# Moving splits and low parts among the units of a first mixer, with three neighbouring instructions swapped elsewhere

## The chip, the cores and the metric

One core of a Trainium2 chip runs the whole program as one launch. The metric is the device time of that launch in microseconds, the median of the runs shown.

## The reference

One layer of a bidirectional encoder for 512 tokens of 1024 channels. After an RMS norm one projection gives the inputs of two mixers and two gates; the mixers' outputs are projected, gated, summed, projected again and added to the input. Then an expert stage follows (16 experts, each takes its 64 best tokens), and a last norm. What the change touches is the first mixer, grouped-query attention with 8 query heads and 2 key heads of 64 channels:

```
h = rms_norm(x, norm1_g[l])
z = jnp.einsum('bsd,dn->bsn', h, w_in[l])
qa, ka, va, qb, kb, vb, ga, gb = jnp.split(z, splits, axis=-1)
...
s = jnp.einsum('bqkgd,bskd->bkgqs', qb, k).astype(jnp.float32)
p = jax.nn.softmax(s, axis=-1).astype(v.dtype)
return jnp.einsum('bkgqs,bskd->bqkgd', p, v)
```

## The kernel before, in words

**Numbers in two parts.** Large products are made of three matmuls: a float32 operand is split into a high part, rounded by ScalarE (ACT), and a low part, the rest, subtracted by VectorE (DVE). A product is high by high, high by low, low by high (`split_product`, L1158 to L1160). The weights w_in come in strips of 128 columns. A strip is loaded by the sync engine (SP) into a ring of four places, `split_hi` (ACT, L795) writes its high part, `split_lo` (DVE, L1878) its low part and counts `w_split` up. The load of a later strip into the same place waits for that count (`load_strip`, L568).

**The first mixer** runs as 32 units `u`, one for each head and each tile of 128 queries. Every engine has its own loop over the units:

- TensorE (PE, L1384): in its unit u the scores of unit u+2 (`scores_a`, L1315), in units 9, 17 and 25 a value product (`values_a`, L1357), then some steps of a column product (`fill`), then the turn, that is four transposes of the softmax rows of unit u (`turn_probs`, L1345).
- ACT (L917): the exponential of unit u (L879), then the read of the turned rows of unit u-2 (L891), then extras.
- DVE (L1998): the maximum of unit u's scores (L2001), then the reciprocal and scaling of unit u-1 (`norm_probs`, L1971 and L1973), then extras.

So DVE's unit u can begin as soon as PE has made the scores in its own unit u-2, and PE's turn of unit u waits for the normalisation in DVE's unit u+1.

**Column groups.** The steps of `fill` prepare queries and keys of the second mixer. There are seven groups of eight steps (three matmuls each); group g multiplies by strip 12+g. `A_FILL` (L469) says how many steps are done after each unit: groups 0 to 6 end in units 0, 5, 10, 15, 20, 25 and 30. The first step of a group waits for the low part of its strip, and for the bank it writes to be emptied (`col_steps`, L1218, through `wait_split` and `pp_take`). Group 2 starts with the second step of unit 5, groups 3, 4, 5 and 6 in units 10, 16, 21 and 26.

**The extras.** Once a group is full, its two heads are emptied: `high_col` on ACT (L902) writes a head's high part, `low_col` on DVE (L1980) its low part; a query head is one piece on each, a key head two pieces (DVE L1993, L1994). Further extras are the splits of the strips 14 to 19 and, four times, the output tile (`read_o`, `low_o`, DVE L1977). The tables `O_READ`, `O_LOW` and `A_LOWS` (L470, L471) name the units of the output tile and of the splits' low parts. The splits' high parts were placed by two conditions in the loop on ACT (L931 to L934).

**Other places.** Ahead of the mixer DVE writes the low parts of h (`low_hT`, L1871) and splits the first strips. The key heads of the first mixer get their low parts by `low_k` (L1918). Behind both mixers and the gates, tiles get their residual added (`add_residual`, L2094) and are routed (`route_max`, `route_norm`).

Of the kernel before, what the change touches and what calls it, by code (L numbers as in the profile page):

```python
# [38 lines left out]
KC = D // P  # L39
# [24 lines left out]
RING = 4  # L64
# [20 lines left out]
def encoder_block(nc, x, norm1_g, w_in, b_gates, q_norm_g, k_norm_g, w_o_a, w_o_b, w_out, norm2_g,  # L85
# [138 lines left out]
    with ExitStack() as ctx:  # L224
# [140 lines left out]
        NA = A_HEADS * NT  # L365
# [101 lines left out]
        N_COL_A = 2 * NG + 1  # L467
        A_LEAD = 6
        A_FILL = [min(N_COL_A * KC, A_LEAD + 2 + (i + 1) * (N_COL_A * KC - A_LEAD - 2) // (NA - 1)) for i in range(NA)]  # L469
        O_READ, O_LOW = (10, 19, 26), (11, 21, NA)  # L470
        A_LOWS = (2, 6, 10, 16, 20, 26)  # L471
        B_HIGHS, B_LOWS = (NA + 4, NA + 6, NA + 7), (NA + 6, NA + 7, NA + 8)
        B_FILL = ([2, 3, 4, 5, 7, 8, 8, 8], [3, 6, 7, 8, 11, 14, 16, 16])

# [15 lines left out]
        def filled_at(plan, g):  # L490

            return next(i for i, steps in enumerate(plan) if steps >= KC * (g + 1))

        def q_of(hp, hh, g):

# [268 lines left out]
        def _(act_):  # L764
# [19 lines left out]
            def split_hi(n):  # L784

                home, before = raw_home(n), before_in_home(n, part_home)
                arrived = sum(2 if strips[m][0] == "wo" else 1 for m in range(n + 1) if raw_home(m) == home)
                act_.wait_ge(w_raw_in[home], 16 * arrived)
                if part_home(n) != home:

                    act_.wait_ge(pv_done, OA + OB)
                elif before is not None:
                    wait_used(act_, before)
                raw, hi, _ = parts_of(n)
                act_.activation(hi, raw, ACT.Copy).then_inc(w_hi_done, 1)  # L795
# [121 lines left out]
            for u in range(NA + 4):  # L917
                if u < NA:
                    soft_exp(u, SEQ, pp[u % 3][:, :])
                    if u == 3 * NA // 4:  # L920

                        act_.dma_start(dist[:, :, :], distance).then_inc(dist_in, 16)
                if 2 <= u < NA + 2:
                    read_probs(u - 2)
                for g in range(N_COL_A):
                    filled = filled_at(A_FILL, g)
                    if u == (filled + 2 if g < N_COL_A - 1 else NA + 1):
                        high_col(g, 0)
                    if u == (filled + 3 if g < N_COL_A - 1 else NA + 1):
                        high_col(g, 1)  # L930
                    if u == filled + 4 and g < 2 * KC // RING:  # L931
                        split_hi(at[col_groups[g][1:]] + RING)
                if u in (1, 2):
                    split_hi(13 + u)  # L934
                if u in O_READ:
                    read_o(O_READ.index(u))

# [908 lines left out]
        def _(dve):  # L1846
# [21 lines left out]
            def low_hT(c):  # L1868
                dve.wait_ge(hT_hi_done, pieces_done(c))
                cols = slice(P * c, P * c + P)  # L1870
                dve.tensor_tensor(hT_lo[:, :, cols], turned_two[c % 2], hT_hi[:, :, cols].bitcast(F32),  # L1871
                                  ALU.subtract).then_inc(hT_lo_done, 1)
# [13 lines left out]
            low_hT(1)  # L1886
            norm_x(3)
            low_hT(2)
            low_hT(3)
            for n in range(2, 6):  # L1890
                split_lo(n)


# [24 lines left out]
            def low_k(kv):  # L1918

                dve.wait_ge(a_hi_done, a_read("k", kv))  # L1920
                half, other = halves_of(kv)
                src, high = tp[K_BANK][half, :], kA[half, kv, 0, :].bitcast(F32)
                dve.tensor_tensor(kA[half, kv, 1, :], src, high, ALU.subtract).then_inc(a_lo_done, 1)
                dve.tensor_tensor(kA[other, kv, 0, :], src, high, ALU.subtract).then_inc(a_lo_done, 1)
# [38 lines left out]
            low_q(2)  # L1963
            low_k(0)
            low_q(3)
            low_k(1)


            def norm_probs(u, width):
# [10 lines left out]
            def low_col(g, hh):  # L1980

                _, kind, grp, hp = col_groups[g]
                dve.wait_ge(col_hi_done, 2 * g + hh + 1)
                src = bank[bank_of[N_TOK + g]]
                half = slice(HD * hh, HD * hh + HD)
                other = slice(HD - HD * hh, 2 * HD - HD * hh)
                if kind == "q":
                    q = q_of(hp, hh, grp)
                    last = dve.scalar_tensor_tensor(q[other, :], src[half, :], SCALE / SLOPES[2 * hp + hh],
                                                    q[half, :].bitcast(F32), ALU.mult, ALU.subtract)  # L1990
                else:
                    hi = kB[half, hh, grp, 0, :].bitcast(F32)
                    dve.tensor_tensor(kB[other, hh, grp, 0, :], src[half, :], hi, ALU.subtract)  # L1993
                    last = dve.tensor_tensor(kB[half, hh, grp, 1, :], src[half, :], hi, ALU.subtract)  # L1994
                if hh:
                    last.then_inc(proj_read_dve, 1)

            for u in range(NA + 5):  # L1998
                if u < NA:
                    dve.wait_ge(score_done, u + 1)  # L2000
                    dve.tensor_reduce(column(nmax, u), pp[u % 3][:, :], AX, ALU.max, negate=True)\  # L2001
                        .then_inc(nmax_done, 1)
                if 1 <= u <= NA:
                    norm_probs(u - 1, SEQ)
                for g in range(N_COL_A):
                    filled = filled_at(A_FILL, g)
                    if u == (filled + 3 if g < N_COL_A - 1 else NA + 2):
                        low_col(g, 0)
                    if u == (filled + 4 if g < N_COL_A - 1 else NA + 3):
                        low_col(g, 1)  # L2010
                if u in A_LOWS:
                    split_lo(14 + A_LOWS.index(u))
                if u in O_LOW:
                    low_o(O_LOW.index(u))
# [99 lines left out]
            def route_norm(c):  # L2114

                dve.wait_ge(sexp_done, c + 1)
                settle(dve.reciprocal(sinv[:, c:c + 1], ssum[:, c:c + 1]))
                dve.tensor_scalar(aff[:, c, :], logit[:, c, :], sinv[:, c:c + 1], None, ALU.mult)\
                    .then_inc(aff_done, 1)


            def low_xn(c, h):

                dve.wait_ge(xn_hi_done, c + 1)
                cols = slice(SEQ * h, SEQ * h + SEQ)
                dve.tensor_tensor(xn_lo[:, c, cols].rearrange("p (k i) -> p k i", k=HALF),
                                  x2[:, c, cols].rearrange("p (i k) -> p k i", k=HALF),
                                  xn_hi[:, c, cols].rearrange("p (k i) -> p k i", k=HALF).bitcast(F32),
                                  ALU.subtract).then_inc(xn_lo_done, 1)
# [18 lines left out]
            route_max(1)  # L2148
            read_h2(2)
            low_xn(0, 1)  # L2150
            route_norm(0)
            add_residual(1, 3)
            low_xn(1, 0)
            low_xn(1, 1)
            read_h2(3, NT, HALF, KC - 2)
# [274 lines left out]
```

## Time and profile before

| | |
|---|---|
| three runs, median (lowest, highest) | 868.34 us (866.88, 869.37) |
| the profiled execution's own time | 867.77 us |
| its span, first to last instruction | 865.8 us |
| mean granted TensorE clock | 0.998 |
| PE busy | 842.6 us, 97% |
| DVE busy | 373.4 us, 43% |
| ACT busy | 264.1 us, 31% |

The page of the profile gives busy times for the whole span and groups instructions by line. The list of waits says for each engine what ended its idle time. The timeline lists single instructions or runs of equal ones in order of time; a number in square brackets behind one is the idle time of its engine just before it and what ended it. A busy PE is one whose records cover the time: matmuls overlap, so a record is longer than the distance to the next one. PEld are the weight loads of TensorE. All times are us from the span's start.

### The profile page before, as it was taken

The page shows a single profiled execution, that of the slowest core. Times are in us where ns is not written, and L with a number is a line of the kernel's source. Part 1 is how long each engine was busy: PE and PEld are TensorE (multiplying, and loading weights), DVE is VectorE, ACT ScalarE, POOL GpSimd, SP SyncE. Part 2 cuts the span into 40 slices and gives each one's busy share as a digit, 9 for nine tenths or more (in the row PEclk, how much of TensorE's full clock was granted, in tenths as well). Part 3 has the DMA queues.
Part 4 walks back from the last instruction along what each step waited for, and adds up shares of the span by engine and source line. Part 5 has one row for each costly group of instructions (what it writes and reads, how often), then busy time and mean ns, then how long its engine had stood idle before and what let it go on. Part 6 is the DMA issues. An engine that isn't in the chain of part 4 may idle for free.

```text
span 865.8 us, 10447 instructions
## 1 busy us (share of the span) xinstructions
PE 842.6 (97%) x4229; PEld 513.7 (59%) x4229; DVE 373.4 (43%) x648; ACT 264.1 (31%) x461; POOL 29.0 (3%) x50
## 2 busy tenths in 40 slices
PE   9999999999999999999999999999999998989996
PEld 8898766787878888888534343344433433334332
DVE  5377977676616245427322236223231311321351
ACT  6233866685624234216011010010100101001231
POOL 1050000000000000003000000000000000000010
PEclk9999999999999999999999999999999999999999
DMA  9730112023034335884899999999999999999995
GB/s 286 175 98 1 49 49 98 24 72 104 27 122 131 95 87 146 305 372 163 333 410 418 425 426 430 424 428 428 424 431 428 427 430 425 430 427 428 429 410 236
DMA packets 81428, 239.20 MB, mean 276 GB/s; under 512 B 8039, under 2 KB 63463, under 8 KB 66789
## 3 DMA queue, kind: packets, MB, share of 16 engines
q1 hardware_dynamic: 75952, 235.94, 69.2%
q10 hardware_dynamic: 5284, 2.09, 1.0%
q8 instruction: 34, 0.56, 0.3%
q0 software_dynamic: 144, 0.51, 0.1%
q14 instruction: 14, 0.11, 0.0%
HBM read 235.92 MB, written 2.62 MB: 276 GB/s over the span
## 4 chain that ended last, share of the span: by engine, by line
PE 82%; DMA 12%; DVE 3%; ACT 1%; issue 1%; POOLq 0%; POOL 0%; SPq 0%; ACTq 0%; DVEq 0%
PE psum L1645 18%; PE psum L1158 11%; PE psum L1677 11%; PE psum L1159 11%; PE psum L1160 11%; DMA wslot<-in_w_down 7%; DMA wslot<-in_w_up 4%; PE psum L1602 3%; PE psum L1696 2%; PE psum L1345 2%; PE psum L1357 2%; PE psum L1805 2%; PE psum L1331 2%; PE psum L1315 1%; PE psum L1164 1%; PE psum L1610 1%
## 5 line engine op out<-in xcount | busy, mean ns | idle before, releaser
L1645 PE MATMUL psum<-wslot,xinT 128*64 128x512 f32 x1000 | 222.4, 595 | 5.8 <-DMA wslot<-in_w_up 3.8
L1645 PEld LDWEIGHTS psum<-wslot,xinT 128*64 128x64 f32 x1000 | 69.8, 137 | 143.5 <-issue 132.1
L1677 PE MATMUL psum<-wslot,actT 128*64 128x512 f32 x424 | 96.0, 597 | 5.0 <-DMA wslot<-in_w_down 5.0
L1158 PE MATMUL psum<-hT_hi,w_hi 128*128 128x512 f32 x208 | 82.9, 399 | 0.0
L1160 PE MATMUL psum<-hT_hi,w_lo 128*128 128x512 f32 x208 | 81.2, 390 | 0.0
L1159 PE MATMUL psum<-hT_lo,w_hi 128*128 128x512 f32 x208 | 81.2, 390 | 0.0
L1878 DVE TENSOR_TENSOR w_lo<-w_raw,w_hi 128x1024 fp32r<-128x1024 f32 (+1 forms) x46 | 52.9, 1174 | 44.8 <-ACT w_hi L795 44.7
L1677 PEld LDWEIGHTS psum<-wslot,actT 128*64 128x64 f32 x424 | 29.2, 137 | 61.4 <-issue 57.4
L1091 ACT ACTIVATE actT<-psum 128x512 f32<-128x512 f32 x16 | 9.6, 597 | 174.4 <-PE psum L1657 174.4
L2283 DVE TENSOR_TENSOR x<-x,psum 128x512 f32<-128x512 f32 x48 | 29.7, 681 | 57.8 <-PE psum L1696 57.8
L2273 DVE TENSOR_TENSOR y_lo<-psum,y_hi 64x512 fp32r<-64x512 f32 x28 | 19.3, 689 | 81.1 <-ACT y_hi L1101 80.7
L795 ACT ACTIVATE w_hi<-w_raw 128x1024 fp32r<-128x1024 f32 (+1 forms) x46 | 45.2, 1017 | 16.3 <-PE psum L1160 16.3
L1158 PEld LDWEIGHTS psum<-hT_hi,w_hi 128*128 128x128 f32 x208 | 39.1, 188 | 10.1 <-issue 2.6
L1160 PEld LDWEIGHTS psum<-hT_hi,w_lo 128*128 128x128 f32 x208 | 39.0, 188 | 8.4
L1159 PEld LDWEIGHTS psum<-hT_lo,w_hi 128*128 128x128 f32 x208 | 39.1, 188 | 7.4
L1086 ACT ACTIVATE act<-psum,slot_vals 128x512 f32<-128x512 f32 x16 | 11.0, 687 | 93.3 <-PE psum L1645 93.3
L2260 DVE SCALAR_TENSOR_TENSOR act<-psum,slot_vals,act 128x512 f32<-128x512 f32 x16 | 12.0, 750 | 59.2 <-ACT act L1086 59.1
L891 ACT ACTIVATE pT<-psum 128x512 f32<-128x512 f32 x48 | 28.5, 596 | 23.6 <-PE psum L1345 13.3
L1101 ACT ACTIVATE y_hi<-psum 64x512 fp32r<-64x512 f32 x28 | 16.5, 589 | 57.3 <-PE psum L1677 57.0
L1602 PE MATMUL psum<-xn,pick 128*128 128x512 f32 x120 | 29.4, 396 | 0.0
L2226 DVE TENSOR_TENSOR xinT<-psum,small 128x512 f32<-128x512 f32 x15 | 9.7, 686 | 40.0 <-PE psum L1610 40.0
L2266 DVE SCALAR_TENSOR_TENSOR act<-act,slot_fac,psum 128x512 f32<-128x512 f32 x16 | 12.0, 747 | 32.8 <-PE psum L1645 32.8
(281 smaller groups left out, 1300.6 us busy)
## 6 DMA issues: line engine op xcount, KB each, us to landing
wslot<-in_w_up SPq DMA_DIRECT2D x27, 2048.0 KB, 25.3
wslot<-in_w_gate SPq DMA_DIRECT2D x25, 2048.0 KB, 26.7
wslot<-in_w_down SPq DMA_DIRECT2D x24, 2048.0 KB, 23.7
w_raw<-in_w_in SPq DMA_DIRECT2D x34, 512.0 KB, 4.3
wslot<-in_w_gate SPq DMA_DIRECT2D x12, 1024.0 KB, 9.5
wslot<-in_w_up SPq DMA_DIRECT2D x9, 1024.0 KB, 11.8
wslot<-in_w_down SPq DMA_DIRECT2D x9, 1024.0 KB, 7.7
w_raw<-in_w_out SPq DMA_DIRECT2D x8, 512.0 KB, 4.7
```

The source lines that it names most:

```text
L795: act_.activation(hi, raw, ACT.Copy).then_inc(w_hi_done, 1)
L891: last = act_.activation(pT[:, head % 2, :, cols], tp[(0, 3)[u % 2]][:, :].rearrange("p (k i) -> p k i", i=P), ACT.Copy)
L1158: pe.matmul(out_, s_hi, m_hi, start=(k == 0), stop=False)
L1159: pe.matmul(out_, s_hi, m_lo, start=False, stop=False)
L1160: return pe.matmul(out_, s_lo, m_hi, start=False, stop=(k == n_k - 1))
L1331: mm = pe.matmul(dst, q_of(head // 2, head % 2, g)[:, cols], keys, start=(v == 0), stop=(v == 1))
L1602: mm = pe.matmul(bank[6 + f][:, :], pick[:, c, :, :], part[:, c, cols], start=(c == 0 and part is xn_hi), stop=(c == NT - 1 and part is xn ...
L1645: mm = pe.matmul(bank[2 * e + n][CAP * f:CAP * f + CAP, :], xinT[:, HALF * h + k, CAP * e:CAP * e + CAP], wslot[place_of(m)][:, k % PART, ...
L1677: mm = pe.matmul(bank[4 + e][CAP * f:CAP * f + CAP, :], actT[:, e, k, CAP * h:CAP * h + CAP], wslot[place_of(m)][:, k % PART, SEQ * f:SEQ ...
L1878: dve.tensor_tensor(lo, raw, hi.bitcast(F32), ALU.subtract).then_inc(w_split, 1)
L2273: dve.tensor_tensor(y_lo[rows, cols], bank[4 + e][CAP * f:CAP * f + CAP, :], y_hi[rows, cols].bitcast(F32), ALU.subtract).then_inc(y_lo_do ...
L2283: dve.tensor_tensor(part, part, bank[added_bank(c, f)][:, :], ALU.add).then_inc(added, 1)
```

## The change

The loops of ACT and DVE get a common rule for when a group's heads are emptied, and the splits get tables of their own:

```diff
-        O_READ, O_LOW = (10, 19, 26), (11, 21, NA)
-        A_LOWS = (2, 6, 10, 16, 20, 26)
+        O_READ, O_LOW = (10, 20, 26), (12, 22, NA)
+        A_HIGHS, A_LOWS = (5, 8, 13, 18, 23, 28), (7, 11, 17, 21, 26, NA + 1)
...
+        def col_read(g, hh):
+
+            if g == N_COL_A - 1:
+                return NA + 1
+            return filled_at(A_FILL, g) + 2 + hh * (1 if g == N_COL_A - 2 else 2)
...
                 for g in range(N_COL_A):
-                    filled = filled_at(A_FILL, g)
-                    if u == (filled + 2 if g < N_COL_A - 1 else NA + 1):
+                    if u == col_read(g, 0):
                         high_col(g, 0)
-                    if u == (filled + 3 if g < N_COL_A - 1 else NA + 1):
+                    if u == col_read(g, 1):
                         high_col(g, 1)
-                    if u == filled + 4 and g < 2 * KC // RING:
-                        split_hi(at[col_groups[g][1:]] + RING)
-                if u in (1, 2):
-                    split_hi(13 + u)
+                if u in A_HIGHS:
+                    split_hi(14 + A_HIGHS.index(u))
...
             low_hT(2)
+            split_lo(2)
             low_hT(3)
-            for n in range(2, 6):
+            for n in range(3, 6):
                 split_lo(n)
...
             low_q(3)
-            low_k(1)
...
                 for g in range(N_COL_A):
-                    filled = filled_at(A_FILL, g)
-                    if u == (filled + 3 if g < N_COL_A - 1 else NA + 2):
+                    if u == col_read(g, 0) + 1:
                         low_col(g, 0)
-                    if u == (filled + 4 if g < N_COL_A - 1 else NA + 3):
+                    if u == (col_read(g, 1) + 1 if g < N_COL_A - 1 else NA + 3):
                         low_col(g, 1)
+                if u == 2:
+                    low_k(1)
...
+            add_residual(1, 3)
             route_norm(0)
-            add_residual(1, 3)
```

The second head of a group that ends in unit f is now emptied in ACT's unit f+4 and DVE's unit f+5, where it was f+3 and f+4. The low parts of strips 14 to 19 stood in DVE's units 2, 6, 10, 16, 20, 26 and stand in 7, 11, 17, 21, 26 and 33. PE's own list of instructions is the same before and after, apart from line numbers, and so are those of POOL and SP.

The first place is DVE's units 6 and 7. A unit begins with L2001 (now L2004), `probs_a_71` is normalised in unit 6 and `probs_a_69` in unit 7, and `w_lo` is a split's low part. Before:

```order
L2001 TENSOR_REDUCE small<-psum 128x1
L1971 RECIPROCAL small<-small 128x1
L1973 TENSOR_SCALAR probs_a_71<-probs_a_71,small 128x512
L1878 TENSOR_TENSOR w_lo<-w_raw,w_hi 128x1024
L2001 TENSOR_REDUCE small<-psum 128x1
L1971 RECIPROCAL small<-small 128x1
L1973 TENSOR_SCALAR probs_a_69<-probs_a_69,small 128x512
L2001 TENSOR_REDUCE small<-psum 128x1
```

And now:

```order
L2004 TENSOR_REDUCE small<-psum 128x1
L1974 RECIPROCAL small<-small 128x1
L1976 TENSOR_SCALAR probs_a_71<-probs_a_71,small 128x512
L2004 TENSOR_REDUCE small<-psum 128x1
L1974 RECIPROCAL small<-small 128x1
L1976 TENSOR_SCALAR probs_a_69<-probs_a_69,small 128x512
L1881 TENSOR_TENSOR w_lo<-w_raw,w_hi 128x1024
L2004 TENSOR_REDUCE small<-psum 128x1
```

Before, the split was strip 15's, and strip 14's stood in unit 2. Now it is strip 14's, one unit's three instructions further on.

The second place is PE's unit 5 in the changed kernel, from the scores of unit 7 to the turn of unit 5, with the semaphores waited for:

```order
L1318 MATMUL psum<-kA,qA 128x512 [waits exp_done]
L1318 MATMUL psum<-kA,qA 128x512
L1161 MATMUL psum<-hT_hi,first_hi 128x512
L1162 MATMUL psum<-hT_lo,first_hi 128x512
L1163 MATMUL psum<-hT_hi,first_lo 128x512
L1161 MATMUL psum<-hT_hi,w_hi 128x512 [waits proj_read_dve,w_split]
L1162 MATMUL psum<-hT_lo,w_hi 128x512
L1163 MATMUL psum<-hT_hi,w_lo 128x512
L1348 MATMUL psum<-ident,probs_a_71 128x128 [waits pT_done,probs_normed]
```

Nothing moved here: the sixth row is the first matmul on strip 14 and waits for the count of split strips, before as now.

The third place is DVE from unit 23 to unit 25, where `kB` are the low parts of a key head of group 4. Before:

```order
L1993 TENSOR_TENSOR kB<-psum,kB 64x512
L1994 TENSOR_TENSOR kB<-psum,kB 64x512
L2001 TENSOR_REDUCE small<-psum 128x1
L1971 RECIPROCAL small<-small 128x1
L1973 TENSOR_SCALAR probs_a_71<-probs_a_71,small 128x512
L1993 TENSOR_TENSOR kB<-psum,kB 64x512
L1994 TENSOR_TENSOR kB<-psum,kB 64x512
L2001 TENSOR_REDUCE small<-psum 128x1
L1971 RECIPROCAL small<-small 128x1
L1973 TENSOR_SCALAR probs_a_69<-probs_a_69,small 128x512
```

And now:

```order
L1996 TENSOR_TENSOR kB<-psum,kB 64x512
L1997 TENSOR_TENSOR kB<-psum,kB 64x512
L2004 TENSOR_REDUCE small<-psum 128x1
L1974 RECIPROCAL small<-small 128x1
L1976 TENSOR_SCALAR probs_a_71<-probs_a_71,small 128x512
L2004 TENSOR_REDUCE small<-psum 128x1
L1974 RECIPROCAL small<-small 128x1
L1976 TENSOR_SCALAR probs_a_69<-probs_a_69,small 128x512
L1996 TENSOR_TENSOR kB<-psum,kB 64x512
L1997 TENSOR_TENSOR kB<-psum,kB 64x512
```

The second head's two pieces moved behind the normalisation of unit 24 (`probs_a_69`).

## Rows read from the trace of the kernel before

**Rows 1.** The page, part 1: busy time, share of the span, instructions

```profile
PE 842.6 (97%) x4229; PEld 513.7 (59%) x4229; DVE 373.4 (43%) x648; ACT 264.1 (31%) x461; POOL 29.0 (3%) x50
```

**Rows 2.** Waits of PE and of PEld, 20 to 250: total, times, longest

```profile
PE psum L1345 <- DVE probs_a L1973: 1.3, 2, 1.1
...
PEld psum L1345 <- DVE probs_a L1973: 3.6, 7, 1.5
```

**Rows 3.** Timeline, 20 to 27: start, length, engine, line, instruction

```profile
20.36 1.22 DVE L1871 TENSOR_TENSOR hT_lo<-psum,hT_hi 128x1024 fp32r<-128x1024 f32 x1 [1.36 <-ACT hT_hi L781]
...
21.50 4.62 DVE L1878 TENSOR_TENSOR w_lo<-w_raw,w_hi 128x1024 fp32r<-128x1024 f32 x4
...
23.89 1.12 PE L1265 MATMUL psum<-first_lo,hT_hi 128*128 128x256 f32 x8
...
24.86 1.12 PE L1270 MATMUL psum<-first_hi,hT_lo 128*128 128x256 f32 x8
...
26.17 0.50 PE L1158 MATMUL psum<-w_hi,hT_hi 128*128 128x512 f32 x1 [0.20 <-DVE w_lo L1878]
```

**Rows 4.** Timeline, 89 to 92: DVE's first reduction, PE up to the turn of unit 0

```profile
89.36 1.29 DVE L2001 TENSOR_REDUCE small<-psum 128x1 f32<-128x512 f32 x2
...
90.78 0.39 PE L1159 MATMUL psum<-hT_lo,first_hi 128*128 128x512 f32 x1
...
91.01 0.39 PE L1160 MATMUL psum<-hT_hi,first_lo 128*128 128x512 f32 x1
...
91.64 0.66 PE L1345 MATMUL psum<-ident,probs_a 128*128 128x128 f32 x4 [0.24 <-DVE probs_a L1973]
```

**Rows 5.** Timeline, 99 to 103: scores of unit 7, strip 14's first matmul, DVE

```profile
99.81 0.71 PE L1315 MATMUL psum<-kA,qA 128*128 128x512 f32 x2
...
100.38 1.22 DVE L1878 TENSOR_TENSOR w_lo<-w_raw,w_hi 128x1024 fp32r<-128x1024 f32 x1
...
101.05 0.39 PE L1158 MATMUL psum<-hT_hi,w_hi 128*128 128x512 f32 x1
...
101.52 0.68 DVE L2001 TENSOR_REDUCE small<-psum 128x1 f32<-128x512 f32 x1
...
102.31 0.49 DVE L1973 TENSOR_SCALAR probs_a<-probs_a,small 128x512 f32<-128x512 f32 x1
```

**Rows 6.** Timeline, 125 to 126: DVE's normalisation of unit 16, strip 16's first matmul

```profile
125.31 0.49 DVE L1973 TENSOR_SCALAR probs_a<-probs_a,small 128x512 f32<-128x512 f32 x1
...
125.88 0.40 PE L1158 MATMUL psum<-hT_hi,w_hi 128*128 128x512 f32 x1
```

**Rows 7.** Timeline, 138 to 149: units 21 to 24 on DVE and PE

```profile
138.89 0.68 DVE L1977 TENSOR_TENSOR oT_lo<-psum,oT_hi 128x512 fp32r<-128x512 f32 x1
...
139.98 0.39 PE L1158 MATMUL psum<-hT_hi,w_hi 128*128 128x512 f32 x1
...
142.57 0.69 DVE L1993 TENSOR_TENSOR kB<-psum,kB 64x512 fp32r<-64x512 f32 x1 [0.61 <-ACT kB L914]
...
145.24 0.62 PE L1345 MATMUL psum<-ident,probs_a 128*128 128x128 f32 x4
...
146.62 0.39 PE L1160 MATMUL psum<-hT_hi,w_lo 128*128 128x512 f32 x1
...
148.07 0.66 PE L1345 MATMUL psum<-ident,probs_a 128*128 128x128 f32 x4 [1.06 <-DVE probs_a L1973]
```

**Rows 8.** Timeline, 166 to 168: DVE behind the last unit of the mixer

```profile
166.28 1.39 DVE L1989 SCALAR_TENSOR_TENSOR qB_next<-psum,qB_next 64x512 fp32r<-64x512 f32 x2 [1.49 <-ACT qB_next L910]
```

**Rows 9.** The page, part 6: DMA issues, size of one, us to landing

```profile
w_raw<-in_w_in SPq DMA_DIRECT2D x34, 512.0 KB, 4.3
```

**Rows 10.** Timeline, 397 to 399: DVE around the last tile's residual

```profile
397.63 0.15 DVE L2117 RECIPROCAL small<-small 128x1 f32<-128x1 f32 x1
...
397.96 0.41 DVE L2094 TENSOR_TENSOR x<-x,psum 128x256 f32<-128x256 f32 x1
```

**Rows 11.** Sums from 360 us on: length; PE, PEld, DVE, ACT, POOL busy; PEclk, DMA share, GB/s

```profile
360.00:866.00 506.00, 486.09 (x2364) 226.01 (x2362) 155.57 (x290) 77.27 (x129) 13.09 (x28) 1.00 0.95 399
```

## The prediction

> **What bounds the kernel now.** I read the page first. TensorE (PE) is busy for 842.6 of 865.8 us [rows 1], so only what it waits for, or issues more slowly for, can be won or lost. The change touches no PE instruction and no transfer; it moves work on VectorE (DVE) and ScalarE (ACT). So the second view was the list of waits, for PE and for its weight loads (PEld), between 20 and 250 us. One releaser stands out: the normalisation of the softmax rows on DVE, line 1973. PE itself is shown idle for it twice, 1.3 us in all, and its weight loads seven times, 3.6 us in all [rows 2]. The third view was the timeline at each of these places, PE beside DVE.
>
> The reader is to compare starts there, not idle columns. Within one group of column products the matmuls of 512 columns start 0.23 us apart, though each is shown as 0.39 us long [rows 4, 7]: the records overlap. At 148.07 us the transposes are shown with 1.06 us of idle before them; the matmul ahead of them started at 146.62, so they could have started at 146.85, and 1.22 us were lost [rows 7]. By idle columns the change can win back 1.1 us at this place and 0.2 at each of the two of [rows 3, 4]; by starts 1.2, 0.34 and 0.40. I go by starts. The Trainium skill ("Perfetto Trace Analysis", opening note) holds against the idle columns that matmuls are pipelined and their busy time is a bad measure; by its rule the sum stands as below, by the idle columns it would come out 0.5 us slower.
>
> **The change, part by part.** All is measured against the profiled execution, 867.77 us; the median of the three runs shown is 868.34, and I carry the sum over to it.
>
> *Swap at the start.* DVE idles 1.36 us before the low parts of the last tile of h [rows 3]. One split takes 1.16 us (four in 4.62), and the split of strip 2 now goes into that hole. The three left end 1.16 us earlier, at about 25.0 instead of 26.1. PE's group of eight matmuls started at 23.89 and the next at 24.86, 0.97 apart, so the product after them could start at 25.83; it started at 26.17 [rows 3]. I take back 0.34 us; bounds 0.2 (the idle shown) and 0.4. If the split ran past the hole, hT_lo would be late by what is over, at most 0.2.
>
> *Low parts of the second key head.* The reduction of unit 0 starts at 89.36 [rows 4], right behind the two pieces of these low parts, which now come two units later. PE's turn of unit 0 could have started at 91.01 + 0.23 = 91.24 and started at 91.64: 0.40 us back. In unit 2 these pieces (two of 0.69 us, by the like pieces of a column group [rows 7]) stand where a split of 1.2 us stood, and the key head is first used in unit 6, so I cost them at nothing there; were that cover gone, 0.2.
>
> *The splits, and what is late next.* This part decides. Column group 2 is the first that multiplies by strip 14. Its first matmul is the second step of unit 5 and waits for that strip's low parts. Those stood in DVE's unit 2; now they come at the end of DVE's unit 7, behind the normalisation of unit 6. PE takes its instructions in their order, so behind that wait stand the turn of unit 5 and all scores after unit 7.
> The time of the split comes out of the rows. Before, a split ran at 100.38 and the reduction of unit 7 followed at 101.52 [rows 5]. With that split gone the reduction waits for its scores, which end at 99.81 + 0.71 = 100.52. From reduction to normalisation it is 102.31 - 101.52 = 0.79 us, and the next instruction follows 0.41 us later (the end of the normalisation less some overlap), so the split starts at about 101.75 and ends 1.22 us later at 102.97. PE stood ready at 101.05 [rows 5]. New wait: about **2.0 us**. The 0.4 us of unit 0 shift both sides alike. Bounds: 1.5 if ACT and DVE gain on PE meanwhile, 2.4 if the high parts (in ACT's unit 5 now) come behind an exponential.
> Strip 16 goes the same way: PE's first matmul on it stood at 125.88. The split now follows the normalisation that started at 125.31 [rows 6], so it runs from 125.72 to 126.94: **1.1 us**, bounds 0.5 and 1.4. Strip 17: the split now stands where the low parts of the output tile stood, at 138.89, and ends at 140.11; PE's matmul stood at 139.98 [rows 7]: **0.2 us**, bounds 0 and 0.5. The splits of strips 15 and 18 fall into stretches where PE does a value product (16 matmuls, in units 9 and 25) and DVE runs ahead; I cost them at nothing, and up to one split, 1.2 us, if that cover fails.
> The output tile's low parts move one unit on and stand directly ahead of a key group's. DVE is then one split (1.15 us from start to next start) later at 142.57, where it had 0.61 us of idle [rows 7]; 0.5 us remain, and the turn at 145.24, which was just on time, comes **0.5 us** late. After that the high parts of the group's second head stand on ACT ahead of the read that the value product of unit 25 needs: two pieces, which I take at 0.6 each, about as long as DVE's [rows 7]. No row shows how much of this is hidden; between 0 and 1.2 I take **0.5 us**, since the turn of unit 24 ahead of it is no longer late and leaves less room than it did.
>
> *Two heads emptied two units apart.* This is what removes the old wait: unit 24 on DVE loses its 1.4 us of key low parts, the normalisation comes that much earlier and the turn at 148.07 is in time: 1.22 us back. The smaller lates among the seven [rows 2] give back 0.2 together. Next late there is the value product, as just said.
>
> *The last split of the row (strip 19)* moves behind unit 32. DVE idles 1.49 us there [rows 8], a split is 1.2, and its product comes 5 us later: nothing. *Loads:* the sync engine's loads of strips 18 to 23 wait for the splits of strips 14 to 19 and go out up to 20 us later. They take 4.3 us [rows 9]. The first, strip 18's, goes out at 103 and is read in ACT's unit 23, near 143 [rows 7]; the last, strip 23's, goes out near 168 and is read in the second mixer's ninth unit, eight units of at least 2 us later (estimate from the units' spacing in [rows 5, 7]). So nothing; no other queue is passed.
>
> *Residual before routing.* The residual add of the last tile started at 397.96, behind a reciprocal and a scaling that began at 397.63 [rows 10]; PE's transposes of that tile follow it. It can move up by 0.33 us at most, less what its own product needs to end: 0.1 us back, bounds 0 and 0.3. The routing of the first tile, now behind it, is wanted only by the last of the routing steps.
>
> **Sum:** back 0.34 + 0.40 + 1.22 + 0.2 + 0.1 = 2.26; new 2.0 + 1.1 + 0.2 + 0.5 + 0.5 = 4.3; together +2.0 us. After the mixer it passes on whole: the expert stage has the DMA engines at 0.95 [rows 11], but its stream is released by PE's progress behind the mixer and shifts with it (bound: 0.5 us absorbed). That is 867.77 + 2.0 = 869.8 for the profiled execution and **870.3** against the median.
>
> **Rivals.** A measurement of this kernel tells about 0.3% from no change, 2.6 us; slower by that is above 870.9.
> - *The lateness carries on* (slower). DVE does not get its place back before unit 24, and the wait of 1.22 us comes back beside the new ones: +3.2, 871.6. For it: the same two engines serve all of it. Against: unit 24 has no extra work left. It decides from the point where DVE is over 1.4 us late in unit 24. Chance 0.18.
> - *Only strip 14 waits.* Once PE has stood for 2 us, DVE and ACT are ahead, and the four waits after it (2.3 us) vanish: 2.0 - 2.26 = -0.3, 868.1. Against: DVE cannot run ahead of PE's scores, which it reduces. Chance 0.15.
> - *The splits are in time* (faster). The change then only removes waits: -2.3, 866.1. It needs DVE 2 us earlier at strip 14 than the rows allow. Chance 0.05.
> - *The clock falls.* At the granted clock of 1.00, which is 2.4 GHz, [rows 11], matmuls start 0.23 us apart; at the other level, 1.2 GHz, it would be 0.46, so each us of work would cost one more, and 3 us of work (an estimate of how long) would give 873.3. The idle 1.06 us [rows 7] lowered it nowhere that the rows show; 2 us have no row. The Trainium skill ("TensorE: Matmul & The Clock Gate", Part 1: The HAM clock gate) has the throttled state as the default that activity releases, which speaks against every longer wait. Chance 0.02.
>
> **How the numbers follow.** The likeliest case, the sum, has 0.60; its own range from the bounds is 869.3 to 871.4. The range 867.8 to 872.0 takes in "only strip 14" and "carries on" and leaves out the rest. Slower by over 0.3%: a fifth of the first case (0.12), most of the second (0.16) and the clock, 0.30. Faster: 0.05 and a bit of "only strip 14", 0.06. Within: 0.64.
>
> **What would show it.** In the profile after: PE's first matmul on strip 14 with about 2 us of idle, released by the split's low parts, one on strip 16 with about 1 us; the turn of unit 0 no longer idle, the turn of unit 24 on time; the first product behind the start's four token groups without idle. No wait on a split in PE's list, or the old 1.2 us still at unit 24, would prove the working wrong.

## The result, and the profile after

| | before | changed |
|---|---|---|
| median | 868.29 us (22 runs) | 870.75 us (22 runs) |
| lowest and highest | 866.53, 870.11 | 868.32, 874.77 |
| ratio, with its 95% interval | | 1.0032 (1.0021 to 1.0044) |
| the profiled execution, its span | 867.77, 865.8 us | 869.63, 867.7 us |
| mean granted TensorE clock | 0.998 | 0.995 |

One disturbed run of the changed kernel (3030.91 us) is in the median, which is 870.69 without it, and left out of the other rows. The forecast was 870.3 us. The kernel became slower by 0.32% by the ratio, whose interval lies above 1; by the medians it is 2.46 us, just under the 2.6 us that the prediction called no change.

The lower mean clock of the changed kernel's profile is no sign of the waits in the mixer. The granted clock is 1.00 around them in this execution and 0.67 between 708 and 712 us, in the expert stage, where it is 1.00 in the trace of before; and the lower level, 1.2 GHz, at which both traces end, lasts 4.7 us here and 3.0 before.

The page of the changed kernel, part 1, which answers to [rows 1]:

```profile
PE 844.1 (97%) x4229; PEld 513.8 (59%) x4229; DVE 373.9 (43%) x648; ACT 264.4 (30%) x461; POOL 29.0 (3%) x50
```

Busy time hardly tells the two apart. The list of waits does, 20 to 250 us, to be read against [rows 2]. Lines moved: the transposes of the turn are L1348 now, the column products L1161 to L1163, the value product L1360, the splits' low parts L1881:

```profile
PEld psum L1161 <- DVE w_lo L1881: 4.4, 3, 2.6
...
PE psum L1161 <- DVE w_lo L1881: 3.1, 2, 2.2
...
PEld psum L1348 <- DVE probs_a L1976: 1.3, 4, 0.5
...
PEld psum L1360 <- ACT pT L897: 1.0, 1, 1.0
...
PE psum L1360 <- ACT pT L897: 0.6, 1, 0.6
```

The two idle spots of PE ahead of the turn [rows 2] are gone. In their place PE waits twice for a split, 3.1 us in all, and once for ACT's read of turned rows ahead of the value product, 0.6.

The timeline at strip 14, which answers to [rows 5]:

```profile
98.90 1.06 ACT L801 ACTIVATE w_hi<-w_raw 128x1024 fp32r<-128x1024 f32 x1
...
99.80 0.68 DVE L2004 TENSOR_REDUCE small<-psum 128x1 f32<-128x512 f32 x1
...
99.85 0.69 ACT L885 ACTIVATE probs_a<-psum,small 128x512 f32<-128x512 f32 x1
...
99.98 0.40 PE L1163 MATMUL psum<-hT_hi,first_lo 128*128 128x512 f32 x1
...
100.66 0.16 DVE L1974 RECIPROCAL small<-small 128x1 f32<-128x1 f32 x1 [0.17 <-ACT probs_a L885]
100.86 0.48 DVE L1976 TENSOR_SCALAR probs_a<-probs_a,small 128x512 f32<-128x512 f32 x1
...
101.26 1.22 DVE L1881 TENSOR_TENSOR w_lo<-w_raw,w_hi 128x1024 fp32r<-128x1024 f32 x1
...
102.53 0.50 PE L1161 MATMUL psum<-hT_hi,w_hi 128*128 128x512 f32 x1 [2.16 <-DVE w_lo L1881]
```

PE's last matmul ahead of strip 14 started at 99.98, so the next could have started at 100.21 and started at 102.53: 2.32 us lost. The split's low part itself takes what it took before; it is only placed behind a normalisation that ends late. One reason why it ends late is the split's high part on ACT (98.90): the exponential that the reciprocal waits for starts right behind it (99.85).

The later places, which answer to [rows 6, 7]: strip 16 at 128.54, strip 17 at 142.72, the turn of unit 23 at 148.30, that of unit 24 at 149.96, the value product at 151.60:

```profile
126.87 0.49 DVE L1976 TENSOR_SCALAR probs_a<-probs_a,small 128x512 f32<-128x512 f32 x1
...
127.27 1.22 DVE L1881 TENSOR_TENSOR w_lo<-w_raw,w_hi 128x1024 fp32r<-128x1024 f32 x1
...
128.54 0.50 PE L1161 MATMUL psum<-hT_hi,w_hi 128*128 128x512 f32 x1 [0.90 <-DVE w_lo L1881]
...
142.72 0.50 PE L1161 MATMUL psum<-hT_hi,w_hi 128*128 128x512 f32 x1
...
146.82 1.06 ACT L801 ACTIVATE w_hi<-w_raw 128x1024 fp32r<-128x1024 f32 x1
...
148.30 0.66 PE L1348 MATMUL psum<-ident,probs_a 128*128 128x128 f32 x4
...
149.66 0.59 ACT L920 ACTIVATE kB<-psum 64x512 fp32r<-64x512 f32 x1
...
149.96 0.60 PE L1348 MATMUL psum<-ident,probs_a 128*128 128x128 f32 x4
...
150.96 0.59 ACT L897 ACTIVATE pT<-psum 128x512 f32<-128x512 f32 x1
...
151.60 1.94 PE L1360 MATMUL psum<-pT,vA 128*64 128x512 f32 x8 [0.58 <-ACT pT L897]
```

The turn of unit 24, which stood idle for 1.06 us in [rows 7], has no wait. The product behind it waits instead: ACT does the high part of a strip's split (146.82) and the second head's high parts (up to 150.25) ahead of the read at 150.96.

At the places of [rows 3, 4] the loss is gone; the first product behind the start, and the turn of unit 0 with the matmul ahead of it:

```profile
25.89 0.40 PE L1161 MATMUL psum<-w_hi,hT_hi 128*128 128x512 f32 x1
...
90.60 0.40 PE L1163 MATMUL psum<-hT_hi,first_lo 128*128 128x512 f32 x1
...
90.83 0.60 PE L1348 MATMUL psum<-ident,probs_a 128*128 128x128 f32 x4
```

**The ledger.** PE's instruction list is the same in all kernels here. So each PE instruction has a start in the trace of before and one in the other trace, and the difference can be followed along the list. The table gives by how much it grows in each stretch (plus is lost, minus is won, us); the stretches end, by the times of before, at 30, 91.64, 100.8, 101.05, 110, 125.88, 146.6, 148.07, 165, 398.44 and the end. The kernels below the first row are those of the experiments.

| | start | turn 0 | turns 2, 4 | strip 14 | pace behind it | strip 16 | strip 17, turn 23 | turn 24 | value product | residual | rest | span |
|---|---|---|---|---|---|---|---|---|---|---|---|---|
| changed | -0.41 | -0.39 | -0.04 | 2.32 | 0.12 | 1.07 | 0.44 | -1.21 | 0.58 | -0.15 | -0.42 | 1.9 |
| splits in time | -0.35 | -0.39 | 0.18 | -0.01 | 0.01 | 0.00 | -0.25 | -1.05 | 0.00 | -0.18 | -1.26 | -3.3 |
| strip 14 in time | 0.20 | -0.39 | 0.19 | -0.01 | 0.02 | 1.07 | 0.45 | -1.21 | 0.59 | -0.15 | -0.65 | 0.1 |
| late splits alone | 0.47 | 0.00 | 0.02 | 1.97 | 1.71 | 1.05 | 0.17 | 0.00 | -0.01 | 0.00 | 0.12 | 5.5 |
| swaps alone | 2.20 | -0.38 | 1.14 | 0.00 | 0.01 | 0.00 | 0.00 | 0.00 | -0.01 | -0.15 | -0.52 | 2.3 |
| two apart alone | 2.77 | 0.00 | 0.01 | 0.00 | 0.15 | 0.00 | 0.20 | -1.22 | -0.04 | 0.00 | -0.17 | 1.7 |
| swaps, strip 14 in unit 4 | -0.13 | -0.39 | 1.14 | 0.00 | 0.01 | 0.00 | 0.00 | 0.00 | 0.00 | -0.15 | -0.26 | 0.2 |

From the turn of unit 0 to the residual the columns repeat from kernel to kernel within 0.1 us, wherever the order of the work is the same. The first column doesn't: it mixes the swap with the pace at the start (last section). The last but one doesn't either: it lies between -1.26 and 0.12, whether a kernel came to it early or late. A column can hold several steps, that is, single instructions at which the difference jumps; where the text below speaks of a step, it is one of these. So single spans are compared through the columns, and times through their medians.

### The profile page after: what moved, and what is told of

It is laid out like the page before. It is cut to its first block, busy times and chain, and to the rows that moved or that the text cites. A ratio compares the mean times of both kernels' runs of the same rounds, so it can differ in the third digit from the quotient of the medians.

```text
span 867.7 us, 10447 instructions
## 1 busy us (share of the span) xinstructions
PE 844.1 (97%) x4229; PEld 513.8 (59%) x4229; DVE 373.9 (43%) x648; ACT 264.4 (30%) x461; POOL 29.0 (3%) x50
## 4 chain that ended last, share of the span: by engine, by line
PE 85%; DMA 8%; DVE 3%; ACT 2%; issue 1%; POOLq 0%; POOL 0%; SPq 0%; ACTq 0%; DVEq 0%
PE psum L1648 21%; PE psum L1680 11%; PE psum L1161 11%; PE psum L1163 10%; PE psum L1162 10%; DMA wslot<-in_w_down 7%; PE psum L1605 3%; PE psum L1699 3%; PE psum L1348 2%; PE psum L1360 2%; PE psum L1808 2%; PE psum L1334 2%; PE psum L1660 1%; PE psum L1167 1%; PE psum L1613 1%
## 5 line engine op out<-in xcount | busy, mean ns | idle before, releaser
L1161 PE MATMUL psum<-hT_hi,w_hi 128*128 128x512 f32 x208 | 83.2, 400 | 3.1 <-DVE w_lo L1881 3.1
L1163 PE MATMUL psum<-hT_hi,w_lo 128*128 128x512 f32 x208 | 81.2, 390 | 0.0
L1881 DVE TENSOR_TENSOR w_lo<-w_raw,w_hi 128x1024 fp32r<-128x1024 f32 (+1 forms) x46 | 52.9, 1173 | 44.9 <-ACT w_hi L801 44.7
L1161 PEld LDWEIGHTS psum<-hT_hi,w_hi 128*128 128x128 f32 x208 | 39.1, 188 | 14.2 <-DVE w_lo L1881 4.4
L1163 PEld LDWEIGHTS psum<-hT_hi,w_lo 128*128 128x128 f32 x208 | 39.0, 188 | 8.5
L2004 DVE TENSOR_REDUCE small<-psum 128x1 f32<-128x512 f32 x32 | 21.9, 687 | 14.4 <-PE psum L1318 14.1
```

The lines of the kernel that those rows point to most:

```text
L1161: pe.matmul(out_, s_hi, m_hi, start=(k == 0), stop=False)
L1163: return pe.matmul(out_, s_lo, m_hi, start=False, stop=(k == n_k - 1))
L1881: dve.tensor_tensor(lo, raw, hi.bitcast(F32), ALU.subtract).then_inc(w_split, 1)
```

## The experiments

**1. The splits in time.** Theory: the change is slower because its splits come later than PE's first matmul on them, and for nothing else. The changed kernel, with other tables:

```diff
-        A_HIGHS, A_LOWS = (5, 8, 13, 18, 23, 28), (7, 11, 17, 21, 26, NA + 1)
+        A_HIGHS, A_LOWS = (3, 6, 11, 16, 21, 28), (4, 9, 14, 19, 24, NA + 1)
```

> The changed kernel with the splits of strips 14 to 19 in other units: low parts in DVE's units 4, 9, 14, 19, 24 and 33, each ahead of the unit in which the PE first multiplies by the strip; everything else as changed. Late splits (my theory): the waits on w_lo (2.3, 1.1 and 0.2 us) go, and with the low parts out of unit 21 also most of the 0.2 and 0.6 us at the turn of unit 23 and the value product of unit 25; what the change takes away stays away, so this is 2.0 to 2.6 us faster than the kernel before, about 866.0 where that is 868.3. Rival, two heads apart are what costs (DVE and ACT late in other units): the waits move from w_lo to the turns, at least 1.5 us stay, and the time is within 1 us of the kernel before or above. Rival, the loss is in the expert stage (a longer wait for weights, lower clock there): the mixer ends earlier and the end does not follow.

Measured: 865.50 us against 867.48 of before in the same session, ratio 0.9972 (0.9959 to 0.9986). What is left of its waits for DVE and ACT in the mixer (list of waits, 20 to 250 us):

```profile
PEld psum L1348 <- DVE probs_a L1976: 1.3, 3, 0.4
...
PEld psum L1360 <- ACT pT L897: 0.4, 1, 0.4
```

No row of PE itself names either engine. This kernel beats both: with the splits in time the rest of the change wins 2.0 us, by the medians and by the ledger up to the residual, and the late splits are what turned it into a loss.

**2. Only strip 14 in time.** Two entries of the tables, to see whether the later waits stand by themselves or only follow from the first:

```diff
-        A_HIGHS, A_LOWS = (5, 8, 13, 18, 23, 28), (7, 11, 17, 21, 26, NA + 1)
+        A_HIGHS, A_LOWS = (3, 8, 13, 18, 23, 28), (4, 11, 17, 21, 26, NA + 1)
```

> The changed kernel with one split moved: strip 14's high part in ACT's unit 3 and its low part in DVE's unit 4. Late splits: only the first wait, 2.3 us, goes; those on strips 16 and 17 (1.1 and 0.2 us) and the ones behind them stay, so the mixer ends 2.3 us earlier than in the changed kernel and the time is that of the kernel before within 0.7 us (868.3). Rival, the later waits exist only since PE's stand at strip 14 shifted the engines against each other: they go too, and it is 1.5 us or more faster than the kernel before. Rival, the wait is made up later whatever it is: the time stays at that of the changed kernel, 2.5 us above the kernel before.

Measured: 867.76 against 867.48, ratio 1.0005 (0.9991 to 1.0019). Its waits of PE, 20 to 250 us:

```profile
PE psum L1161 <- DVE w_lo L1881: 0.9, 1, 0.9
...
PE psum L1360 <- ACT pT L897: 0.6, 1, 0.6
```

In the ledger strip 16, strip 17 with turn 23, and the value product lose 1.07, 0.45 and 0.59, as in the changed kernel (1.07, 0.44, 0.58). The wait on strip 14 neither hides the later ones nor makes them.

**3. The late splits alone.** The kernel before with the change's tables for the splits and nothing else:

```diff
-        A_LOWS = (2, 6, 10, 16, 20, 26)
+        A_HIGHS, A_LOWS = (5, 8, 13, 18, 23, 28), (7, 11, 17, 21, 26, NA + 1)
...
-                    if u == filled + 4 and g < 2 * KC // RING:
-                        split_hi(at[col_groups[g][1:]] + RING)
-                if u in (1, 2):
-                    split_hi(13 + u)
+                if u in A_HIGHS:
+                    split_hi(14 + A_HIGHS.index(u))
```

> The kernel before with one part of the change alone: the splits' high and low parts at the units of the changed kernel; heads one unit apart, key head, output tiles and the swaps as before. Late splits: all three waits on w_lo stand (2.3, 1.1 and some 0 to 0.2 us) and none of the old ones goes, 1.2 us at the turn of unit 24 included, so it is the slowest of all, 3.0 to 3.8 us above the kernel before (871.3 to 872.1). Rival, two heads apart are what costs: within 1 us of the kernel before.

Measured: 872.85 against 867.48 (6 and 29 runs), ratio 1.0061 (1.004 to 1.0081), that is 5.4 us by the medians, a miss: 3.0 to 3.8 were expected. The waits themselves are as expected: 1.97, 1.05 and 0.17 in the ledger, 3.2 together. What was not expected stands behind the first of them (timeline of PE, and the sums of the stretch 104 to 108: length, PE, PEld, DVE, ACT, POOL busy, PEclk, DMA share, GB/s):

```profile
103.52 0.50 PE L1156 MATMUL psum<-hT_hi,w_hi 128*128 128x512 f32 x1 [1.81 <-DVE w_lo L1876]
...
105.84 0.63 PE L1156 MATMUL psum<-hT_hi,w_hi 128*128 128x512 f32 x1
...
106.27 0.63 PE L1157 MATMUL psum<-hT_lo,w_hi 128*128 128x512 f32 x1
```

```profile
104.00:108.00 4.00, 4.00 (x17) 3.27 (x16) 1.85 (x4) 1.85 (x4) 0.00 (x0) 0.57 0.45 131
```

The matmuls start 0.43 us apart and the granted clock is 0.57 of full speed: for most of this stretch TensorE ran at 1.2 GHz, not 2.4. That is the rival of the falling clock. The column behind strip 14 holds 1.71 us here; 0.12 stand there in the changed kernel, where the clock did not fall, so the fall cost 1.6. Waits and fall make 4.8 of the 5.4 us. Only this one of the six executions has a trace, so it is not shown that the clock fell in the others.

**4. The three swaps alone.** The kernel before with the change's other three hunks (`split_lo(2)` ahead of `low_hT(3)`, `low_k(1)` in DVE's unit 2, `add_residual(1, 3)` ahead of `route_norm(0)`):

```diff
             low_hT(2)
+            split_lo(2)
             low_hT(3)
-            for n in range(2, 6):
+            for n in range(3, 6):
...
-            low_k(1)
...
+                if u == 2:
+                    low_k(1)
...
-            route_norm(0)
             add_residual(1, 3)
+            route_norm(0)
```

> The kernel before with the three other moves alone: strip 2's split ahead of the last tile of h, the second key head's low parts in DVE's unit 2 behind the split that stands there, the last tile's residual ahead of a routing step. By the working: 0.4 us back at the start, 0.4 at the turn of unit 0, 0.15 at the residual, and up to 0.3 lost at the turn of unit 2, where split and key head now stand together: 0.6 to 0.9 us faster than the kernel before (867.5), all of it to be read as steps in the starts of PE's matmuls. Rival, a step won early on is lost again where PE waits for something that does not move (weights): less than 0.3 us.

Measured: 868.10 against 867.48, ratio 1.0008 (0.9995 to 1.0021): a miss. The swap at the start is won (0.46 by its steps, under a slow start that hides it in the first column), the turn of unit 0 (0.38) and the residual (0.15) too, but the turn of unit 2 is lost:

```profile
94.15 0.69 DVE L1924 TENSOR_TENSOR kA<-psum,kA 64x512 fp32r<-64x512 f32 x1
...
94.88 0.70 DVE L1925 TENSOR_TENSOR kA<-psum,kA 64x512 fp32r<-64x512 f32 x1
...
95.60 1.22 DVE L1878 TENSOR_TENSOR w_lo<-w_raw,w_hi 128x1024 fp32r<-128x1024 f32 x1
...
97.65 0.49 DVE L1973 TENSOR_SCALAR probs_a<-probs_a,small 128x512 f32<-128x512 f32 x1
...
98.20 0.66 PE L1345 MATMUL psum<-ident,probs_a 128*128 128x128 f32 x4 [0.69 <-DVE probs_a L1973]
```

Here strip 14's split is still in unit 2, behind the key head's two pieces, and the turn that waits for the normalisation behind them comes 0.84 us late by starts; the turn of unit 4 loses 0.22 more. In the changed kernel the split has left unit 2.

**5. The same swaps with strip 14 in unit 4**, to test just that:

```diff
-        A_LOWS = (2, 6, 10, 16, 20, 26)
+        A_LOWS = (4, 6, 10, 16, 20, 26)
```

> The three swaps on the kernel before as in the run of the three swaps alone, and strip 14's low parts in DVE's unit 4 where that run left them in unit 2. That run gained nothing: in its trace the turn of unit 0 is in time, but the turn of unit 2 is 0.84 us late, since unit 2 on DVE held the key head's two pieces and a split. Theory: the swap's gain hangs on the split's leaving unit 2. Then the turn of unit 2 is within 0.2 us, and the kernel 0.5 to 0.8 us faster than that run and than before, about 867.0 to 867.5 by runs; the trace tells it better than the time, as a measurement holds 1.2 us. Rival: the key head's pieces cost their time wherever they stand, and the loss moves to the turns of units 3 or 4: the same time as that run.

Measured: 867.86 against 867.65, ratio 1.000 (0.9989 to 1.001): the theory as I had put it falls. The turn of unit 2 is in time, and the turn of unit 4 is late by 1.12 us:

```profile
96.71 0.69 DVE L1989 SCALAR_TENSOR_TENSOR qB<-psum,qB 64x512 fp32r<-64x512 f32 x1
...
97.43 1.23 DVE L1878 TENSOR_TENSOR w_lo<-w_raw,w_hi 128x1024 fp32r<-128x1024 f32 x1
...
98.69 0.69 DVE L2001 TENSOR_REDUCE small<-psum 128x1 f32<-128x512 f32 x1
...
100.03 0.66 PE L1345 MATMUL psum<-ident,probs_a 128*128 128x128 f32 x4 [0.97 <-DVE probs_a L1973]
```

Unit 4 holds the first group's second head here (`qB`), and the split is again the second extra. In experiment 1 the heads are two units apart, that piece is in unit 5, the same split stands alone in unit 4, and the turns 2 and 4 lose 0.18 together where they lose 1.14 here. So the outcome is the rival's, the cause is not: it is neither the key head, which stands alone in unit 2 here and costs nothing, nor unit 2. In these units DVE has room for one extra, and a second one makes the turn late. The swaps keep their gain only with the other parts of the change.

**6. The heads two apart alone.** The kernel before with this part, and the output tile one unit later:

```diff
-        O_READ, O_LOW = (10, 19, 26), (11, 21, NA)
+        O_READ, O_LOW = (10, 20, 26), (12, 22, NA)
...
-                    if u == (filled + 3 if g < N_COL_A - 1 else NA + 1):
+                    if u == (filled + (4 if g < N_COL_A - 2 else 3) if g < N_COL_A - 1 else NA + 1):
...
-                    if u == (filled + 4 if g < N_COL_A - 1 else NA + 3):
+                    if u == (filled + (5 if g < N_COL_A - 2 else 4) if g < N_COL_A - 1 else NA + 3):
```

> The kernel before with one part of the change alone: the two heads of a group two units apart, with the output tile's read and low parts one unit later (20, 22); all splits where they stood before. If the old wait at the turn of unit 24 is owed to the second head's two low pieces alone, the 1.22 us there go, and the wait at the value product of unit 25 (0.64 us in the changed kernel) comes only as far as ACT is behind there, at most 0.64: 0.6 to 1.2 us faster than before, about 867 where before stands at 867.5 to 868.3, with no wait on a split. Rival: the lateness at unit 24 is owed to the order of units 21 to 24 as a whole, so that the wait only moves to the turn of unit 23 and the value product: within 0.3 us of before, with 1 us or more of loss at these two.

Measured: 866.70 against 867.65, ratio 0.9989 (0.9977 to 1.000), as the theory had it, though the interval reaches no change and the ledger carries it: 1.22 us won at the turn of unit 24, 0.20 lost ahead of it, nothing at the value product. The 0.20 are 0.42 lost at the turn of unit 20, where a split now stands behind two key pieces in one unit of DVE, less 0.18 won at the turn of unit 19. ACT's second half of the second head, its read, the turn of unit 24 and the value product:

```profile
149.00 0.59 ACT L914 ACTIVATE kB<-psum 64x512 fp32r<-64x512 f32 x1
...
149.97 0.60 PE L1345 MATMUL psum<-ident,probs_a 128*128 128x128 f32 x4
...
150.30 0.59 ACT L891 ACTIVATE pT<-psum 128x512 f32<-128x512 f32 x1
...
150.97 1.51 PE L1357 MATMUL psum<-pT,vA 128*64 128x512 f32 x6
```

The second head's high parts stand ahead of the read, as in the changed kernel, and the product is in time. So the 0.6 us there needs the high part of a split in ACT's unit 23 (146.82 in the trace of the changed kernel); in experiment 1, where that split is in unit 21, the 0.6 us are missing too. That split alone does not make it: experiment 3 has it in unit 23 as well and loses nothing at the product, to which PE comes late, from a turn of unit 24 that still waits 1.06 us.

**7. Two more profiled executions of the changed kernel**, for the clock behind strip 14:

> The changed kernel again, one look. In its first profile the 2.2 us wait on strip 14 left the granted clock at 1.00; in the run with the late splits alone a 1.8 us wait at the same place was followed by 3.4 us at 0.5 (matmuls of 512 columns 0.42 us apart), 1.7 us more. Theory: the clock falls behind this wait in some executions and not in others, so that the changed kernel has executions near 869 and others near 873. Rival: it never falls there in this kernel, and the spread of its times comes from the start and the expert stage. A look with 0.5 between 103 and 110 us speaks for the theory; the same waits as in the first profile (2.3, 1.1, 0.2, 0.2, 0.6 us) are expected either way.

> The changed kernel a third time, as the second look: by the theory the clock falls behind the wait on strip 14 in one of these looks or the other (a chance of a half each, by the two groups of its times), by the rival in none; the five waits stand as before.

Measured: 874.07 and 871.63 us, one time each. The wait on strip 14 is 2.33 us in both, and the other waits are the ledger's within 0.02. Sums of the stretches behind that wait, in the first profile:

```profile
104.00:108.00 4.00, 4.00 (x23) 3.33 (x22) 3.18 (x7) 3.88 (x9) 0.00 (x0) 1.00 0.41 122
```

in the second:

```profile
104.00:108.00 4.00, 2.71 (x10) 2.33 (x11) 1.24 (x2) 1.35 (x4) 0.00 (x0) 0.76 0.38 108
108.00:112.00 4.00, 4.00 (x21) 3.20 (x19) 3.18 (x7) 3.12 (x7) 0.00 (x0) 0.81 0.09 27
```

and in the third:

```profile
104.00:108.00 4.00, 4.00 (x16) 3.23 (x14) 2.02 (x5) 2.78 (x6) 0.00 (x0) 0.57 0.43 124
```

The clock fell behind the wait in two profiles of three; no trace of a kernel without this wait shows a fall between 100 and 112 us. The pace column of the ledger is 1.71 and 1.68 there and 0.12 in the first, so a fall costs 1.6 us. The second execution also lost 2.34 us at the start. Of the 21 times of the changed kernel seven lie between 872.07 and 874.77, above the highest of before (870.11) and of experiment 2 (870.92), which has no such wait. These seven do not count the falls: the third execution (not one of the 21), with a fall and no loss at the start, took 871.63 and lies below them, and the second needed both for its 874.07. How often the clock falls is not shown beyond these three profiles, nor why it fell in two of them and not in the first.

## Why the prediction was right, and where it was not

- **Swap at the start**, 0.34 us back: the product starts 0.36 earlier and the next matmul 0.10 more, in each of the kernels with the swap. Confirmed. The 0.41 of the first column agrees with it by luck: in the kernels with the same swap that column holds -0.41 to 2.20.
- **Turn of unit 0**, 0.40 back: 0.39. Confirmed. The key head's pieces cost nothing in unit 2, as predicted, because the split has left it; the price put on the loss of that cover, 0.2, was wrong: experiment 4, where the split is still there, loses 0.84 at the turn of unit 2.
- **Strip 14**, 2.0 new: 2.32, and 0.11 at the next matmul. The working took 0.79 us from reduction to normalisation, from the one row it had [rows 5]; here it is 1.06 (99.80 to 100.86). The reciprocal waited for ACT's exponential, whose sum it takes, and that stood behind the split's high part. The upper bound (2.4) was for the reverse order, the high parts behind an exponential; the sum had no term for this.
- **Strip 16**, 1.1: 1.07, and 0.10 at the next matmul. **Strip 17 and the turn of unit 23**, 0.2 + 0.5: 0.18 and 0.10 at strip 17, 0.22 at the turn. The 0.44 of their column agrees with neither term, as it also holds the next matmul of strip 16 and the win at the turn of unit 19. The turn was priced at over twice its loss.
- **Turn of unit 24**, 1.22 back: 1.21. That the starts and not the idle column (1.06) are to be counted is borne out.
- **Value product**, 0.5 new: 0.58. The size was right and the cause half right: it takes the split on ACT as well, not the head's high parts alone (experiment 6).
- **Smaller lates**, 0.2 back: 0.18 at the turn of unit 19, here and in every kernel with the heads two apart. **Residual**, 0.1 back: 0.15.
- **Signs**: the five that the prediction named (idle ahead of strips 14 and 16, none at the start's product and at the turn of unit 0, the turn of unit 24 on time) stand in the profile after.
- **Sum**: predicted +2.0, by the ledger 2.3 up to the residual and 1.9 at the end of the profiled execution. The terms miss by up to 0.4 us, in both directions, and part of that cancels. "After the mixer it passes on whole, bound 0.5 absorbed" stays open: the column behind the residual is -0.42 here, but -1.26 in experiment 1, which came to it early, and 0.12 in experiment 3, which came latest. Against the median: 870.3 predicted, 870.75 measured; how much of that gap is falls of the clock, which the sum has not, is not shown.
- **Rivals.** "Lateness carries on": the turn of unit 24 has no wait, it fell. "Only strip 14 waits": the four losses after it stand (strips 16 and 17, the turn of unit 23, the value product), it fell. "The splits are in time" is not what the change does; made so by experiment 1, the change gains 2.0 us against before in the same session, where that rival had 2.3. "The clock falls" had a chance of 0.02 and is real: in two profiles of three. The step that failed is "2 us have no row", read as "unlikely". Its price was also off: 3 us were assumed, without a row, and the falls cost 1.6. The page of the Trainium skill held against the long waits ("TensorE: Matmul & The Clock Gate", Part 1: The HAM clock gate) has the throttled state come back with idleness; the granted clock of 0.57 behind a wait of 2.2 us in the third profile agrees, and 1.00 behind the same wait in the first profile shows that one profile does not settle it.

So the forecast's mechanism was right and its total low, by 0.3 us in the ledger and 0.45 against the median. The waits, less what is won, give 2.3 us, the clock adds 1.6 in some executions, and the medians differ by 2.46.

## What to carry to other kernels

A split that is moved into a "free" unit must be checked against the first matmul that waits for it, not against how busy its own unit is. In this kernel, whose PE is 97% busy, two extras in one of DVE's units made a turn late in three places (experiments 4 to 6), so a move can be worth nothing alone (the swaps in experiment 4) and keep its gain beside others (the same swaps in experiment 1). A new wait of 2 us on TensorE cost its own length here and, in some executions, 1.6 us more by the clock.

## What was not expected of the hardware

The pace at the start. TensorE's first matmuls of 512 columns (`g_row`, four of them) with the sums of a stretch behind them, in the trace of before and then in that of the swaps alone:

```profile
5.61 2.17 PE L1280 MATMUL psum<-g_row,ones 1*128 1x512 f32 x4
```

```profile
8.00:12.00 4.00, 3.85 (x34) 3.69 (x34) 3.96 (x4) 3.27 (x6) 0.20 (x1) 1.00 1.02 392
```

```profile
5.60 3.78 PE L1280 MATMUL psum<-g_row,ones 1*128 1x512 f32 x4
```

```profile
8.00:12.00 4.00, 4.00 (x14) 2.69 (x13) 3.12 (x4) 1.21 (x2) 0.00 (x0) 1.00 1.02 392
```

The same four matmuls take 3.78 us where they took 2.17, and in the next stretch 14 matmuls are begun where the trace of before has 34. Behind the four, matmuls of 128 columns start 0.21 us apart where they start 0.11 apart in the trace of before. Yet the granted clock is shown as 1.00. That is no reading: the trace's records of the clock begin at 13.65 us here and at 6.03 us in before, and a stretch ahead of the first record is shown as 1.00. The records begin late, at 13.65 to 13.92 us, in three executions (the swaps alone, two apart alone, the second of the changed kernel), and these are the three whose start column holds 2.20 to 2.77 us; in all others they begin at 5.3 to 6.2. What the clock was ahead of the first record is not shown; the distance between starts shows the slow pace. This moves an execution by some 0.3%, which is why the columns behind the start, and medians over runs, carry the argument here. The Trainium skill ("TensorE: Matmul & The Clock Gate", Part 1: The HAM clock gate) calls the slow start of a kernel's matmuls "run-variable"; these traces agree, with up to 2.8 us between executions.
